# Cache attention of a decode step with the queries as stationary operand in four 32-column tiles and the pages moving, scores in one row per sequence, head and query

## The reference

```python
def sparse_attend(q, k_sel, v_sel, q_pos, k_pos_sel, rel_bias):
    logits = jnp.einsum('bqhd,bqkhd->bhqk', q, k_sel).astype(jnp.float32) * (HEAD_DIM ** -0.5)
    rel = q_pos[None, :, None] - k_pos_sel
    bias = jnp.moveaxis(rel_bias.astype(jnp.float32)[t5_bucket(rel)], -1, 1)
    logits = jnp.where((rel >= 0)[:, None], logits + bias, MASK_VALUE)
    p = jax.nn.softmax(logits, axis=-1).astype(v_sel.dtype)
    return jnp.einsum('bhqk,bqkhd->bqhd', p, v_sel)
```

## Time and profile before

| | us |
|---|---|
| timed runs: median of 3 (lowest to highest) | 2400.01 (2397.11 to 2400.71) |
| profiled execution: from the first to the last instruction (span) | 2385.6 |
| key stage (500.9 to 789.2) | 288.3 |
| softmax stage (789.2 to 836.0) | 46.8 |
| value stage (836.0 to 1066.7) | 230.7 |

### The profile page before, as it was taken

The page is one execution under the profiler, slowest core; times in us unless marked ns, Lnnn a source line. Parts: engine busy times, 40 slices in busy tenths (PEclk is TensorE's granted clock), DMA queues, the critical chain, the costliest instruction groups (busy, mean ns, idle before and its releaser), DMA issues.

```text
span 2385.6 us, 44903 instructions
## 1 busy us (share of the span) xinstructions
PE 2241.6 (94%) x15229; PEld 2166.7 (91%) x15229; DVE 1278.0 (54%) x2474; ACT 937.0 (39%) x1657; POOL 156.7 (7%) x301
## 2 busy tenths in 40 slices
PE   5949999889999499999999999999999999999997
PEld 5926889779999399998999999999999999999997
DVE  4313999624434678785555445555445554445553
ACT  5423433333233222226444445444334443334443
POOL 3410000021111111100000000000000000000012
PEclk9969999889999699999999999999999999999999
DMA  8440446245555157753555654555555555555542
GB/s 234 116 85 0 116 118 168 77 155 180 181 167 180 64 182 224 228 179 106 143 156 142 184 137 136 150 148 152 144 155 144 156 141 157 142 157 142 144 138 79
DMA packets 541471, 346.35 MB, mean 145 GB/s; under 512 B 19331, under 2 KB 520363, under 8 KB 541008
## 3 DMA queue, kind: packets, MB, share of 16 engines
q1 hardware_dynamic: 514480, 259.88, 40.4%
q0 software_dynamic: 25824, 84.47, 10.8%
q10 hardware_dynamic: 1088, 1.05, 0.1%
HBM read 335.24 MB, written 10.83 MB: 145 GB/s over the span
## 4 chain that ended last, share of the span: by engine, by line
PE 82%; DVE 6%; issue 4%; DMA 2%; ACT 2%; POOLq 1%; POOL 1%; DVEq 0%; SPq 0%; ACTq 0%
PE psG L1295 21%; PE psG L1296 21%; PE psG L1297 21%; PE psS L1292 11%; PE psT L1289 3%; PE psM L1292 2%; DVE rt L991 2%; DMA bias_scratch<-gsb 1%; DVE WL L868 1%; DVE Ws L982 1%; POOLq L417 1%; PE psM L1296 1%; PE psM L1297 1%; PE psM L1295 1%; POOL ikst L421 1%
## 5 line engine op out<-in xcount | busy, mean ns | idle before, releaser
L868 DVE TENSOR_TENSOR WL<-RAW,WH 128x512 fp32r<-128x512 f32 x1008 | 681.5, 691 | 767.4 <-ACT WH L535 755.2
L535 ACT ACTIVATE WH<-RAW 128x512 fp32r<-128x512 f32 x1008 | 624.6, 630 | 893.4 <-PE psG L1297 842.0
L1295 PE MATMUL psG<-XH,WH 128*128 128x320 f32 (+1 forms) x2688 | 851.8, 317 | 13.0 <-DVE WL L868 6.9
L1296 PE MATMUL psG<-XL,WH 128*128 128x320 f32 (+1 forms) x2688 | 838.8, 312 | 0.0
L1297 PE MATMUL psG<-XH,WL 128*128 128x320 f32 (+1 forms) x2688 | 836.9, 311 | 0.0
L1295 PEld LDWEIGHTS psG<-XH,WH 128*128 128x128 f32 x2688 | 507.5, 189 | 21.1 <-DVE WL L868 10.8
L1296 PEld LDWEIGHTS psG<-XL,WH 128*128 128x128 f32 x2688 | 508.3, 189 | 0.8
L1297 PEld LDWEIGHTS psG<-XH,WL 128*128 128x128 f32 x2688 | 507.4, 189 | 0.0
L1295 PE MATMUL psG<-MH,WH 128*128 128x320 f32 x960 | 300.9, 313 | 0.3 <-DVE ML L1264 0.3
L1297 PE MATMUL psG<-MH,WL 128*128 128x320 f32 x960 | 295.8, 308 | 0.0
L1296 PE MATMUL psG<-ML,WH 128*128 128x320 f32 x960 | 295.7, 308 | 0.0
(11 more groups left out here) (314 smaller groups left out, 1900.3 us busy)
## 6 DMA issues: line engine op xcount, KB each, us to landing
RAW<-in_w_in SPq DMA_DIRECT2D x160, 512.0 KB, 4.9
RAW<-in_w_ffn_gate SPq DMA_DIRECT2D x88, 512.0 KB, 4.6
RAW<-in_w_ffn_up SPq DMA_DIRECT2D x88, 512.0 KB, 4.6
RAW<-in_w_ffn_down SPq DMA_DIRECT2D x80, 512.0 KB, 4.2
kst<-in_cache_k POOLq DMA_DIRECT2D x64, 512.0 KB, 3.5
vst<-in_cache_v POOLq DMA_DIRECT2D x64, 512.0 KB, 3.9
RAW<-in_w_out SPq DMA_DIRECT2D x32, 512.0 KB, 5.0
RAW<-in_w_attn_br SPq DMA_DIRECT2D x16, 512.0 KB, 4.1
```

The source lines that it names most:

```text
L535: act.activation(WH[:, s % 2, 4 * r:4 * r + 4], RAW[:, s, 4 * r:4 * r + 4], ACT.Copy).then_inc(hi_done, 1)
L868: dve.tensor_tensor(WL[:, s % 2, k], RAW[:, s, k], WH[:, s % 2, k].bitcast(F32), ALU.subtract).then_inc(lo_done, 1)
L1295: pe.matmul(out, WH[:, s % 2, k], hi, start=start, stop=False)
L1296: pe.matmul(out, WH[:, s % 2, k], lo, start=False, stop=False)
```

## The change

The roles of the operands are exchanged in both products with the pages, and pages are taken in pairs: one of each of two sequences (a table of pages in the new order, ptab2).

The queries, eight a head, are stored in qsz with 24 columns of zeros around them, so that the four heads of a half add up into 32 rows. A score matmul has 32 stationary columns and moves 128 keys; the tile r of four (sequence r // 2, half of the heads r % 2) writes 32 rows of PSUM, so 128 rows hold two sequences, eight heads and eight queries, and a row holds all keys of one query. L has such a row for each of four groups of two sequences, 1024 cached and 64 new keys wide. The scores' bias is then one number a row, except on the last page. The mask product (pairM by sel, fp32r) gives each row its unpicked keys; the maximum and the sum are taken along the row, the sum by the exp itself. The weights are turned back, page by page, 32 columns of L are the stationary operand of a value matmul, and 512 columns of a page's values move. ScalarE divides (osb), TensorE turns and ScalarE sorts the output into oT. The loops `cz` on TensorE and `ga` on TensorE, ScalarE and VectorE are written out. The places in SBUF are new (PLACING). The new keys' scores are 64 matmuls in one block, and TensorE's `values_turned` of the last group stands ahead of the sums over ub.

```diff
+LW = PAST + NS
+ROWS = 2 * H * Q
+B_NEW, B_FAR, B_N = P, P + NS, P + NS + 1
...
+            pool.tensor_copy(ptab2[:].rearrange("o (g n c) -> o g n c", g=B // 2, c=2), ptab[:].rearrange("o (g c n) -> o g n c", g=B // 2, c=2)).then_inc(pt_dn, 1)
...
+            pool.memset(qsz[:], 0.0).then_inc(qz, 1)
...
+            act.wait_ge(qz, 1)
+            for h in range(H):
+                ins = act.activation(qsz[:, h, :, Q * (h % 4):Q * (h % 4) + Q], QK[:, h, NP:NT].rearrange("p (b q) -> p b q", b=B), ACT.Copy)
+            ins.then_inc(qs_dn, 1)
...
-                        act.activation(kTs[:, 0:4, :], TB[0][:].rearrange("p (h n) -> p h n", h=4), ACT.Copy).then_inc(kc_A, 1)
+                        act.activation(kTs[:, j % 2, 0:4, :], TB[0][:].rearrange("p (h n) -> p h n", h=4), ACT.Copy).then_inc(kc_A, 1)
...
-                act.wait_ge(x_sub, t + 1)
-                act.activation(L[:, t], L[:, t], ACT.Exp).then_inc(x_exp, 1)
...
+            def x_soft(g):
+                act.wait_ge(x_max, g + 1)
+                act.activation(L[:, g, :], L[:, g, :], ACT.Exp, bias=stat[:, 24 + g:25 + g], accum_out=stat[:, 28 + g:29 + g]).then_inc(x_exp, 1)
+
...
+
+            def values_scaled(g):
+                act.wait_ge(o_mm, g + 1)
+                act.wait_ge(x_rs, g + 1)
+                if g >= 2:
+                    act.wait_ge(o_tr, g - 1)
+                act.activation(osb[:, g % 2, :], SB[g % 2][:], ACT.Copy, scale=stat[:, 32 + g:33 + g]).then_inc(o_sb, 1)
+
+            def values_out(g):
+                act.wait_ge(o_tr, g + 1)
+                for k in range(4):
+                    src = TB[g % 2][:, P * k:P * k + P].rearrange("p (b h k q) -> p b h k q", b=2, h=2, k=4)[:, :, :, k, :]
+                    ins = act.activation(oT[:, :, SEQ + 2 * Q * g:SEQ + 2 * Q * g + 2 * Q].rearrange("p (h k) (b q) -> p b h k q", k=4, b=2)[:, :, :, k, :],
+                                         src, ACT.Copy)
+                ins.then_inc(o_cp, 1)
 
...
-            for h in range(H):
-                dve.scalar_tensor_tensor(LN[:, :, h, :], SB[0][0:NS, NS * h:NS * h + NS].rearrange("p (b q) -> p b q", b=B), SC,
-                                         biasN[:, h:h + 1, :].to_broadcast([NS, B, Q]), ALU.mult, ALU.add).then_inc(ln_dn, 1)
...
-                    dve.scalar_tensor_tensor(L[:, :, c, :].rearrange("p t o x -> p t (o x)"), SB[s // 2][:].rearrange("p (t x) -> p t x", t=NPG), SC,
-                                             biasS[:].rearrange("p t h q -> p t (h q)"), ALU.mult, ALU.add).then_inc(lg_done, 1)
+                    row = L[:, bass.ds(g, 1), :].rearrange("p o n -> p (o n)")
+                    if s == 1:
+                        dve.tensor_scalar(row[:, 0:512], SB[0][:], SC, biasR[:, B_FAR:B_N], ALU.mult, ALU.add).then_inc(lg_done, 1)
+                    else:
+                        dve.tensor_scalar(row[:, 512:PAST - PAGE], SB[1][:, 0:512 - PAGE], SC, biasR[:, B_FAR:B_N], ALU.mult, ALU.add)
+                        dve.scalar_tensor_tensor(row[:, PAST - PAGE:PAST], SB[1][:, 512 - PAGE:512], SC, biasR[:, 0:P],
+                                                 ALU.mult, ALU.add).then_inc(lg_done, 1)
...
-            for t in range(NPG):
-                row = L[:, t].rearrange("p b (h q) -> p b h q", h=H)
-                ch.step(dve.tensor_tensor(row, row, MS[:, t, :].rearrange("p (b o q) -> p b o q", b=B, o=1).to_broadcast([P, B, H, Q]), ALU.add))
...
-            dve.tensor_reduce(mx[:].rearrange("p i x -> p (i x)"), L[:].rearrange("p t b x -> p (b x) t"), AX, ALU.max).then_inc(x_mx, 1)
...
-            for t in range(NPG):
-                row = L[:, t].rearrange("p b x -> p (b x)")
-                dve.tensor_tensor(row, row, MB[1][:], ALU.subtract).then_inc(x_sub, 1)
...
-            dve.tensor_reduce(mx[:].rearrange("p i x -> p (i x)"), L[:].rearrange("p t b x -> p (b x) t"), AX, ALU.add).then_inc(x_sm, 1)
...
-            dve.reciprocal(rS[:].rearrange("p b h q -> p (b h q)"), TB[0][:]).then_inc(x_rs, 1)
...
+                ch.step(dve.tensor_tensor(row[:, 0:512], row[:, 0:512], a[:], ALU.add))
+                ch.step(dve.tensor_tensor(row[:, 512:PAST], row[:, 512:PAST], b[:], ALU.add))
+                dve.tensor_tensor(row[:, PAST:LW], row[:, PAST:LW], SB[0][:, NS * g:NS * g + NS], ALU.add).then_inc(x_ad, 1)
+                ch.wait()
+                dve.wait_ge(x_ad, g + 1)
+                dve.tensor_reduce(stat[:, 24 + g:25 + g], row, AX, ALU.max, negate=True).then_inc(x_max, 1)
...
+                dve.wait_ge(x_pt, g + 1)
+                dve.tensor_copy(L[:, g, 512:PAST], G[1][:]).then_inc(x_pcD, 1)
+                dve.wait_ge(x_exp, g + 1)
+                dve.reciprocal(stat[:, 32 + g:33 + g], stat[:, 28 + g:29 + g]).then_inc(x_rs, 1)
...
-                mm(SB[0][0:NS, NS * h:NS * h + NS], QK[:, H + h, NP:NT], QK[:, h, NP:NT]).then_inc(ln_mm, 1)
+            pe.wait_ge(qs_dn, 1)
+            for g in range(B // 2):
+                for k in range(4):
+                    for r in range(4):
+                        h = 4 * (r % 2) + k
+                        ins = mm(MB[1][32 * r:32 * r + 32, NS * (4 + g):NS * (5 + g)], qsz[:, h, 2 * g + r // 2, :], QK[:, H + h, NP:NT], k == 0, k == 3)
+            ins.then_inc(ln_mm, 1)
...
-                            ins = mm(SB[s // 2][:, NS * t + Q * h:NS * t + Q * h + Q], kTs[:, h, :], qs[:, h, bass.ds(b * Q, Q)],
-                                     t == 0 and h == 0, t == NPG - 1 and h == H - 1)
...
+                        if n % 2 == 0:
+                            continue
+                        if g and t % 4 == 0:
+                            pe.wait_ge(lg_done, 2 * g - 1 + t // 4)
+                        for k in range(4):
+                            for r in range(4):
+                                h = 4 * (r % 2) + k
+                                ins = mm(SB[t // 4][32 * r:32 * r + 32, P * (t % 4):P * (t % 4) + P], qsz[:, h, 2 * g + r // 2, :], kTs[:, r // 2, h, :],
+                                         k == 0, k == 3)
+                        if t % 4 == 3:
+                            ins.then_inc(kq_done, 1)
...
-            mm(TB[0][:], ones[:], mx[:].rearrange("p i x -> p (i x)"), True, False)
-            mm(TB[0][:], ones[0:NS, :], LN[:].rearrange("p b h q -> p (b h q)"), False, True).then_inc(x_den, 1)
...
+                pe.matmul(a[:], sel[:, g, :], pairM[:, 0:512], start=True, stop=True, skip_group_check=True)
+                pe.matmul(b[:], sel[:, g, :], pairM[:, 512:PAST], start=True, stop=True, skip_group_check=True).then_inc(x_mk, 1)
...
+                for t in range(NPG):
+                    tr(G[t // 4][:, ROWS * (t % 4):ROWS * (t % 4) + ROWS], L[:, g, PAGE * t:PAGE * t + PAGE])
+                tr(SB[1][0:NS, ROWS * g:ROWS * g + ROWS], L[:, g, PAST:LW]).then_inc(x_pt, 1)
...
+            def values_turned(g):
+                pe.wait_ge(o_sb, g + 1)
+                if g >= 2:
+                    pe.wait_ge(o_cp, g - 1)
+                for k in range(4):
+                    ins = tr(TB[g % 2][:, P * k:P * k + P], osb[:, g % 2, P * k:P * k + P])
+                ins.then_inc(o_tr, 1)
...
-                            ins = mm(SB[s // 2][:, Q * h:Q * h + Q], vst[:, j, P * h:P * h + P], L[:, t, bass.ds(b, 1), Q * h:Q * h + Q].rearrange("p o q -> p (o q)"),
-                                     t == 0 and h == 0, t == NPG - 1 and h == H - 1)
-                        ins.then_inc(v_used, 1)
...
-                ins = mm(TB[0][:, NS * h:NS * h + NS], vs[:, P * h:P * h + P], LN[:, :, h, :])
...
+                        if g and s == 1 and j == 0:
+                            values_turned(g - 1)
+                        if j % 2 == 0:
+                            continue
+                        if t == 0 and g >= 2:
+                            pe.wait_ge(o_sb, g - 1)
+                        for r in range(4):
+                            ins = mm(SB[g % 2][32 * r:32 * r + 32, :], L[:, g, P * t + 32 * r:P * t + 32 * r + 32], vst[:, j - 1 + r // 2, 512 * (r % 2):512 * (r % 2) + 512],
+                                     t == 0, False)
+                        ins.then_inc(v_used, 2)
+                for r in range(4):
+                    ins = mm(SB[g % 2][32 * r:32 * r + 32, :], PTn[:, g, 32 * r:32 * r + 32], vs[:, 512 * (r % 2):512 * (r % 2) + 512], False, True)
+                ins.then_inc(o_mm, 1)
...
+            for g in range(GN["ga"]):
+                ga(g)
+            values_turned(3)
+
+
             pe.wait_ge(yc_done, CT + 2)
```

More of the change, by code:

```diff
@@ L414, in _, with page @@
             pool.memset(IW[:], 0.0).then_inc(pool_zero, 1)
-            def page(i):
-                return pool.value_load(ptab[0:1, bass.ds(i, 1)], min_val=0, max_val=POOL_PAGES - 1)
+            def page(i, table=ptab):
+                return pool.value_load(table[0:1, bass.ds(i, 1)], min_val=0, max_val=POOL_PAGES - 1)
             with pool.Fori(0, B) as b:
@@ new lines, in _ @@
+            dve.wait_ge(ln_mm, 1)
```

(44 more changed lines are left out.)

199 lines of the change are left out of this document (88 added, 111 removed).

## The result

The changed kernel takes 2276.26 us (median of four, 2273.93 to 2285.05) against 2400.36 for the kernel before in the same session: a ratio of 0.9489, interval 0.9471 to 0.9508. That is 124 us less; the forecast was 71 less, 2329, and its range ended at 2284. The direction was right, the size too small. The profiled execution has a span of 2272.4 us, 113.2 under the 2385.6 of before.

What follows compares the result with a forecast made beforehand. TensorE, busy 94% of the span, bounds key and value stages, VectorE the softmax stage. Ahead of pages +4, bias copies -0.5, key -31.6, softmax -21.5, value -23, behind it +1.4: -71.2 from 2400.0 gives 2329 us, range 2284 to 2366.

Steps and rivals of the forecast that it cites:

- What a pass costs: Score and value blocks: one TensorE pass takes 0.107 us for 128 moving columns, 0.43 us for 512.
- rival 2: Score and value blocks: passes queue as one stream without overlap, 3.42 and 3.44 us a block; 2419 us, chance 0.16.
- How four tiles overlap: Score and value blocks: each matmul advances by one pass, giving 1.9 us a score block and 2.15 a value block.
- The new wait: Key stage: TensorE waits 16 times some 0.8 us for VectorE's copy of the next page's keys, 12.8 us.
- The softmax stage: Between key and value stage: shorter work on sums, maxima and masks gains 21.5 us, with 4 us either way.
- Ahead of the pages: Before the first key page: the block of 64 new-key score matmuls adds 4 us, bounds +2 and +8.
- half overlap: Score and value blocks: the forecast's own case, tiles overlapping by one pass a matmul; 2329 us, chance 0.50.
- The value stage: Value pages with convolution taps: 207.5 us against 230.7, gain 23, TensorE no longer busy throughout and waiting for VectorE's WL.
- One sign that the forecast named: Key or value stage: a fall of the granted clock, 0.99 before, would show the prediction as a whole wrong.
- The sum's base: Whole kernel: 14.4 us lie around the profiled span of 2385.6 us, making the median of 2400.01, and stay unchanged.
- Rival 1: Score and value blocks: four tiles fully side by side, 0.86 us a score block, key stage 222; 2291 us, chance 0.30.
- Rivals 2 and 3: The third: half overlap with tile starts 0.06 us apart, score block 2.7 us; 2355 us, chance counted within 0.50.

Runs made afterwards that it cites:

- half-taps run: Changed kernel with VectorE leaving out 15 of the 31 taps of each convolution channel in the value stage; 2244.52 us, without part of the work.
- one-tile run: Changed kernel with all matmuls of a block on one column tile, from the key stage's second group and the value stage's third; 2354.45 us.
- tile-by-tile run: Changed kernel with only the order of a score block's 16 matmuls changed, the four of one column tile next to each other; 2316.11 us.

## Why the prediction was right or wrong

The forecast missed by 53 us: 33 in the key stage, 7 in the value stage, 3 ahead of the pages, and 10 outside the edited stages.

- **What a pass costs** was right: 0.107 us for 128 columns (0.109 measured), 0.43 for 512 (0.43 on one tile, 0.45 behind a block's first pass), and no overlap would have cost what rival 2 said (3.5 us a block on one tile). **How four tiles overlap** is the step that failed. I took the second pass of a matmul to hold up the next tile, since passes start in the order of the program in every row I read. Those rows had all passes on the same columns, so they could not show what happens between tiles. A pass that waits for its own tile does not hold up the others, until three wait. A score block took 1.0 us instead of 1.9 + 0.1, and a pair 6.62 instead of 7.56: 32 of them make 30 of the 33 us. The Trainium skill (TensorE: Matmul & The Clock Gate, Part 3) is cited there with two sentences; the trace agrees with tiles that run together (some 7 ns between starts by the row of the value block, 4 by the page), and it disagrees with strict program order: that holds within one tile only. The 0.111 in the forecast's sum had 0.004 for the next tile's start, which no row had shown; with 0.007 it would be the same to 0.1 us.
- **The new wait** behind MAX8 and MATCH_REPLACE was rightly placed and counted; it was 0.63 us, not 0.8. That is the other 3 us, and moving the two instructions gave all of it back.
- **The softmax stage**, 25.1 against 25.3 us (a maximum took 1.29 us, an exp 1.20, forecast 1.3 and 1.25), and the end of the value stage, +1.3 against +1.4, came out as worked.
- **Ahead of the pages** +0.6 was measured for the +4 of the sum. The block was costed at half overlap, 5.5 us, where it takes 3.0. Another 1.0 us came from the stretch between the conv state and the first page, at the higher granted clock, which the sum did not have; what that owes to the block is not shown.
- **The value stage**: that VectorE would take over as the bound was right, and the half-taps run shows it. The size was off by three small terms: its taps got a little shorter (482 ns a tap's first half instead of 487, 188.4 instead of 191.25 us busy), its waits were 1.06 instead of 1.3 us, and the 2.5 us that I added because both engines seemed near each other was not needed: with full overlap TensorE lies 29 us below. One sign that the forecast named as speaking against it did come, the granted clock fell there to 0.93; but VectorE's work and its 11.9 us of waits fill the stage, so the lower clock cost at most part of these waits.
- **The sum's base** failed too: "14.4 us lie around the span, and I take them as unchanged." It is 1.5 us. The rest was the difference between one short execution, the profiled one, and the usual ones, and the kernel after shows the short prompt attention in its usual ones.
- Rival 1 had the right mechanism and the key stage to 2 us (222 against 223.8), its gain of 64.5 us to the tenth; that is partly luck, since its wait was 2.8 us too long and its 32 pairs 2.6 us too short (6.54 against 6.62). Its 2291 was 15 too high, by the sum's base and the value stage. Rivals 2 and 3 are excluded by the one-tile run and by the score block's row.

What I gave to half overlap, 0.50, should have gone to full overlap: the only argument against the latter was an order seen where it could not be broken.

## What to carry to other kernels

Small matmuls on disjoint column tiles ran side by side here even though each is two passes, as long as neighbouring matmuls in the program went to different tiles: with four matmuls in a row on one tile the block more than doubled. When an engine is sped up, the next bound is read from the busy time and the waits of the others in that stage, and the waits it leaves can be mere order: here MAX8 ahead of a copy, and a copy ahead of a rounding, were worth 10 and 8 us by moving lines. And compare the profiled span with the time of its own execution, not with the median of others.

## What had not been expected of the hardware

- TensorE starts later passes on a free tile while earlier passes of the program still wait for another tile: three of them, by the starts and the 0.47 us from tile to tile in the tile-by-tile run.
- The loads of the second passes run while the first passes of the same tile are still moving, and beside each other: the eight loads of a value block, 0.11 us each, are over after 0.16 us, and the second passes start only 0.45 us after the first.
- With the same kernel, the stretch at the lower granted clock in the prompt's attention differs between executions by most of 10 us of the whole (mean clock 0.75 and 0.56 over the same 35 us).
